# Index scores of a head pair in two groups of four, with a quarter tile of the projection between them

## The reference, cut to what matters

```
qi = rope_partial(split_heads(qi, N_IDX_HEADS), pos)
ki = rope_partial(ki[:, :, None], pos)[:, :, 0]
...
sc = jnp.einsum('thd,sd->ths', qi, ki) * IDX_DIM ** -0.5
score = jnp.einsum('ths,th->ts', jax.nn.relu(sc), w)
```

## Time and profile before

| what | us |
|---|---|
| median of three runs | 2710.42 |
| the three runs | 2716.11, 2710.42, 2710.17 |
| span of the profiled execution | 2720.3 |
| TensorE busy in it | 2572.7 |
| TensorE's mean granted clock | 0.975 |

### The profile page before, as it was taken

How to read it: one execution, slowest core, us unless ns; L and a number is a source line. 1 busy time by engine, 2 the same in 40 slices (tenths; PEclk the granted TensorE clock), 3 DMA queues, 4 the chain that set the end, 5 groups by cost and what they waited for, 6 DMA issues and landing times.

```text
span 2720.3 us, 52410 instructions
## 1 busy us (share of the span) xinstructions
PE 2572.7 (95%) x16711; PEld 2180.8 (80%) x16711; DVE 994.4 (37%) x1779; ACT 818.7 (30%) x1546; POOL 868.0 (32%) x651
## 2 busy tenths in 40 slices
PE   7999999999999999879999999999999999996997
PEld 2227879899999989779922388898999999896997
DVE  2241346776111234431103423487731122344113
ACT  0012334444333333322200133344433333333221
POOL 5012224334333333334300232343343333342341
PEclk8999999999999999989999999999999999998999
DMA  8983222223333323234478622232233333222443
GB/s 264 346 287 104 55 57 74 73 71 88 90 90 97 80 75 82 59 110 133 151 239 276 214 72 54 63 81 69 74 98 88 93 85 80 76 68 73 136 125 131
DMA packets 410102, 311.75 MB, mean 115 GB/s; under 512 B 21304, under 2 KB 347840, under 8 KB 408712
## 3 DMA queue, kind: packets, MB, share of 16 engines
q1 hardware_dynamic: 382296, 283.35, 35.8%
q10 hardware_dynamic: 27632, 26.21, 3.1%
HBM read 280.81 MB, written 30.92 MB: 115 GB/s over the span
## 4 chain that ended last, share of the span: by engine, by line
issue 56%; PE 20%; POOL 19%; POOLq 2%; DMA 1%; DVE 0%; SPq 0%; DVEq 0%; ACT 0%; ACTq 0%
POOL w_lo L458 18%; PE misc L513 6%; PE proj L572 4%; PE proj L566 4%; PE proj L568 4%; POOL act_lo L451 1%; POOLq L443 1%; POOLq L441 1%; POOLq L465 1%; POOLq L457 0%; PE misc L521 0%; DMA out_y_prompt<-work 0%; PE misc L489 0%; DVE work L1159 0%; DMA raw<-in_w_in 0%
## 5 line engine op out<-in xcount | busy, mean ns | idle before, releaser
L566 PE MATMUL proj<-act_hi,w_hi 128*128 128x288 f32 (+1 forms) x4672 | 1336.6, 301 | 29.2 <-DVE act_lo L1156 20.1
L568 PE MATMUL proj<-act_lo,w_hi 128*128 128x288 f32 (+1 forms) x4672 | 1312.1, 296 | 0.0
L458 POOL TENSOR_TENSOR w_lo<-raw,w_hi 128x512 fp32r<-128x512 f32 (+1 forms) x584 | 778.4, 1336 | 1432.6 <-ACT w_hi L866 1432.4
L572 PE MATMUL proj<-act_hi,w_lo 128*128 128x288 f32 (+1 forms) x4672 | 1004.1, 296 | 0.0
L566 PEld LDWEIGHTS proj<-act_hi,w_hi 128*128 128x128 f32 (+1 forms) x4672 | 883.1, 189 | 58.8 <-issue 48.0
L568 PEld LDWEIGHTS proj<-act_lo,w_hi 128*128 128x128 f32 (+1 forms) x4672 | 883.6, 189 | 3.4
L572 PEld LDWEIGHTS proj<-act_hi,w_lo 128*128 128x128 f32 (+1 forms) x4672 | 752.3, 188 | 0.0
L866 ACT ACTIVATE w_hi<-raw 128x512 fp32r<-128x512 f32 (+1 forms) x584 | 365.6, 629 | 1186.5 <-PE proj L572 1141.9
L513 PE MATMUL misc<-work,sc 128*2 128x512 f32 x768 | 344.8, 607 | 18.7 <-DMA work<-in_w_ada 11.5
L513 PEld LDWEIGHTS misc<-work,sc 128*2 128x2 f32 x768 | 64.2, 86 | 278.6 <-issue 278.3
L451 POOL TENSOR_TENSOR act_lo<-xy,act_hi 128x576 fp32r<-128x576 f32 x32 | 50.2, 1582 | 352.7 <-ACT act_hi L873 296.2
(11 more groups left out here) (169 smaller groups left out, 1695.0 us busy)
## 6 DMA issues: line engine op xcount, KB each, us to landing
raw<-in_w_in SPq DMA_DIRECT2D x448, 256.0 KB, 2.9
work<-in_w_ada SPq DMA_DIRECT2D x96, 1024.0 KB, 5.2
raw<-in_w_out SPq DMA_DIRECT2D x128, 256.0 KB, 2.8
x_keep<-xy ACTq DMA_DIRECT2D x32, 288.0 KB, 2.5
lb<-x_keep SPq DMA_DIRECT2D x24, 288.0 KB, 3.3
x_keep<-xy ACTq DMA_DIRECT2D x4, 1152.0 KB, 11.6
out_y_prompt<-work SPq DMA_DIRECT2D x4, 1024.0 KB, 3.9
qi_raw<-x_keep SPq DMA_DIRECT2D x8, 288.0 KB, 3.8
```

The lines of the kernel that those rows point to most:

```text
L458: pool.tensor_tensor(w_lo[:, c, :, 0:width], raw[:, c, :, 0:width], w_hi[:, c, :, 0:width].bitcast(F32), ALU.subtract)\
L566: pe.matmul(dst, w_hi[:, c, kk, 0:width], act_hi[:, k, cols], start=(k == 0), stop=False)
L568: pe.matmul(dst, w_hi[:, c, kk, 0:width], act_lo[:, k, cols], start=False, stop=False)
L572: m = pe.matmul(proj[b][0:width, half, 0:HALF], w_lo[:, c, kk, 0:width], act_hi[:, k, cols], start=False, stop=(k == KT - 1))
```

## The change

On TensorE alone, `scores` takes a half, products 0 to 3 or 4 to 7. In a query tile the swap product comes after the first quarter in place of the second. Then come two quarters, the first four products, the fourth quarter, and the last four products. In the first recurrent block the swap product stays after the second quarter, and the products are split in the same way around the fourth quarter. There are 8 pairs in each of 2 layers, so 16 places.

```diff
-                def scores(q, first=False):
+                def scores(q, half, first=False):
 
-                    hold(pe, roped, l * 17 + q + 2)
+                    if half == 0:
+                        hold(pe, roped, l * 17 + q + 2)
                     for e, (b, hh) in enumerate((b, hh) for b in (1, 2, 3, 4) for hh in range(2)):
+                        if e // 4 != half:
+                            continue
                         hold(pe, idx_read, l * 64 + (8 * q + e - 3 if not first or e > 3 else 0))
...
                 def query_tile(q, b, use, first=False):
 
-                    chunks(QI + q, b, use, (0, 1))
+                    chunks(QI + q, b, use, (0,))
                     swap(QI - 1 + q, 1 - b, swap_i[:, :], qi_raw, P)
-                    chunks(QI + q, b, use, (2, 3))
+                    chunks(QI + q, b, use, (1, 2))
                     if first:
                         hold(pe, ki_ready, l + 1)
                         hold(pe, t_read, l * T_EV + 2)
-                    scores(q - 1, first)
+                    scores(q - 1, 0, first)
+                    chunks(QI + q, b, use, (3,))
+                    scores(q - 1, 1, first)
...
                     if first:
                         swap(QI + 7, 0, swap_i[:, :], qi_raw, P)
-                    chunks(LRU + 2 * g, 1, g + 4, (2, 3))
+                    chunks(LRU + 2 * g, 1, g + 4, (2,))
                     if first:
-                        scores(7)
+                        scores(7, 0)
+                    chunks(LRU + 2 * g, 1, g + 4, (3,))
+                    if first:
+                        scores(7, 1)
                         hold(pe, idx_read, (l + 1) * 64)
                         t_event(2)
```

## The result

The changed kernel takes 2772.4 us (median of 4 runs, 2766.0 to 2775.2) against 2713.3 us. The ratio is 1.0208, with a 95% interval of 1.0188 to 1.0229. It is slower, as forecast. But the forecast was +39 us with a range up to 2765, and the time lies above that range. Run once more beside the kernel before, it gave 2770.3 against 2717.1 us, ratio 1.0199 (1.0183 to 1.0215), so +53 us. The spans of the profiled executions are 2770.2 and 2768.5 us after, 2720.3 and 2718.0 us before.

A forecast was written before the change was run, and what follows sets the result against it. TensorE's own stream was taken to bound the kernel. Four products 23.8, first tiles 4.5 and clock 11 summed to +39.3 us, giving 2750 us from the median 2710.4, range 2734 to 2765.

The forecast's parts named there:

- The bound: Whole kernel and index-query stages: TensorE's own stream sets the pace, busy 2572.7 of 2720.3 us.
- the tie of product 4 to the end of the fourth quarter: Query tile: product 4 still comes 2.64 us after the last matmul, through ScalarE's fourth upper, copy and first ReLU.
- the four products that lose their cover: Products 0 to 3, moved ahead of the fourth quarter, cost 1.49 us in each of 16 places, +23.8 us.
- The wait of the first tile: First query tile: earlier swap product waits 2.24 us for take_query(0), +4.5 us over two layers.
- The swap product: Steady query tiles: its earlier place costs 0 and gains nothing, since nothing waits for VectorE or the freed bank.
- The faster rival: First four ReLUs run during the fourth quarter, the 16.9 us of waits go away, 2700 us; chance 0.05.
- the clock's term: Gaps before product 4 and in first tiles: 10 clock falls out of 18 gaps at 1.1 us, +11 us.
- the discount from 1.56 to 1.1: A full low-clock stretch costs 1.56 us; taken as 1.1 for overlap with idle time and products 4 to 7.
- The rival with a fall at every gap: All 18 gaps bring the clock down at full price, 28 us, giving 2767 us; chance 0.12.
- the clock would have held: Rival, by the skill's rule: clock stays at 1.00 in the gaps, sum 28.3 us, 2739 us; chance 0.23.

The follow-up runs named there:

- e4_filled: Changed kernel with four matmuls on constant data filling the idle stretch in each of the 16 places; +27.6 us against before, ratio 1.0112.
- e7_first_filled: e1_swap_only with four matmuls on constant data in the wait before the first tile's swap product; +2.4 us against before, ratio 1.0011.
- e2_split_only: Changed kernel with the swap product back after the second quarter; +51.1 us against before, ratio 1.0204.
- e6_late_wait: e3_relus_ahead with swap product back after the second quarter, TensorE's wait for pair 7's ReLUs moved behind tile LRU+1; -19.7 us against before, ratio 0.9927.
- e3_relus_ahead: Changed kernel with ScalarE's first four ReLUs of a pair ahead of the fourth upper, last four behind the copy; -12.2 us against before, ratio 0.9956.
- e1_swap_only: Kernel before with the swap product after the first quarter, eight products together behind the fourth; +12.1 us against before, ratio 1.0047.
- e9_half_filled: e4_filled with two added matmuls in place of four in each place; +34.1 us against before, ratio 1.0135.
- after: The changed kernel, first measurement and profile; 2772.4 us against 2713.3, ratio 1.0208.
- after_again: The changed kernel once more, unaltered, for a second profile; +53.2 us against before, ratio 1.0199.
- before_again: The kernel before once more, unaltered, for a second profile; -1.3 us against before, ratio 0.9989.

## Why the prediction was right and wrong

**What held.** The bound, the tie of product 4 to the end of the fourth quarter (2.64 us before and after), and the four products that lose their cover. Their term was 23.8 us, and e4_filled and e7_first_filled give 2 x 11.88 = 23.8. The wait of the first tile was forecast as 2.24 us a layer and is 2.09 and 2.03. The swap product costs next to nothing else, 0.26 us in a layer. The prediction saw no gain in its earlier place either, but there is one once the products are split: e2_split_only and e6_late_wait show that the old place would have cost some 0.4 us a tile. The faster rival asked for ReLUs ahead of the fourth quarter's end. ScalarE's order excluded them in this change, and where that order was altered, in e3_relus_ahead, they brought the gain.

**What failed: the clock's term.** It was put at 10 falls by 1.1 us, 11 us in all. Measured, in each layer: 1.72 us behind the first tile (e1_swap_only against e7_first_filled), and behind the places the stage of the changed kernel, (166.10 + 172.23 + 170.23 + 169.28) / 4 = 169.46 us, less the 158.91 of e4_filled, so 10.55. Two layers by 12.27 make **24.5 us**. The sum is then 23.8 + 4.1 + 0.5 + 24.5 = 52.9 us, and the runs gave 59 and 53.

The count and the price were both too low. There are 13 gaps with a fall in one profile and 14 in the other, but some lasted two or three times as long, which makes 16 and 19 low stretches for the 10 assumed. One stretch costs about 1.5 us (1.47 behind the places, 1.72 in a first tile), and not 1.1. The step that failed is the discount from 1.56 to 1.1. It says that a low stretch overlaps "the idle time itself and products 4 to 7, which ScalarE paces". But hardly any of it lies in the idle time: in the two profiles of the changed kernel the low stretches begin between 0.4 us before product 4 and 1.4 us after it, for instance at 353.30 with product 4 at 353.43. And ScalarE's pace hides little: unpaced, products 4 to 7 take 1.81 us at the whole clock (e3_relus_ahead), paced 2.16, and at the low clock 3.68, twice the unpaced time. So the full price fell due, 3.61 - 2.09 = 1.52 us by the start of the next quarter.

The clock's term accounts for 13.5 of the 22 us that 2750 was short. With it the sum gives 2710.4 + 52.9 = 2763, which still lies inside the stated range. The other 9 us up to 2772.4 are 3 by which the kernel before came out higher in the comparison itself (2713.3) and 6 that the second comparison, at +53, does not show, and no run says where they lay. The rival with a fall at every gap had the better price, but its 2767 is under the measured time too. Its 18 low stretches are near the 16 and 19 of the traces, though these lie behind 13 and 14 gaps.

The Trainium skill, page "TensorE: Matmul & The Clock Gate", section "Why this matters for your kernels", advises against longer idle gaps than these, by which the clock would have held. The trace does not agree, and the measurement decides: idle stretches of 2.33 us between dense work brought the clock down in 11 and 12 of 16 places.

## What to carry to other kernels

Before moving work out of a wait, ask what ends the wait: if it is another engine's program order, the wait stays where it was and the moved work is simply added. Split both sides of a handshake or neither. And price a longer idle stretch of TensorE twice, once for itself and once for the clock behind it. Here the second was as dear as all the products moved, and matmuls that nobody needs, put in the gap, won back about half of the loss.

## What the runs showed of the hardware

- How the granted clock answers an idle stretch of TensorE that recurs between dense matmuls, in 16 places of a profile: 0.40 us brought no fall (e4_filled); 1.07 us none in the two profiles before, but for behind pair 7, where a second wait of 1.65 us follows and three of four were followed by a fall; 1.36 us one (e9_half_filled); 2.33 us 11 and 12, and 7 in e2_split_only. A single wait of 2.0 to 2.1 us in the first tile was followed by a fall in both layers each time (for instance in after, after_again and e1_swap_only), and one of 2.32 us in e3_relus_ahead in one layer of two.
- A low stretch that was filled with the products was in some places followed by a second one at 1.2 GHz, although TensorE was busy for 3.27 of the first 3.40 us (353.30 to 360.10 above). In others it was not: at 312.4 the same products ran just as long, 3.67 us, and the clock was whole again after 3.40.
- Where the products follow close behind the rotation that they wait for, the first four take 1.72 to 1.81 us for 1.35 (e2_split_only, e6_late_wait). I read it as TensorE's queue, which has five semaphore waits ahead of them and no lead left. No run took the waits apart, so this is argued and not shown.
- The same program differs by some 10 us between executions, and the granted clock goes with it: the 12 runs of before_again lie between 2707.6 us at a clock of 0.980 and 2721.2 us at 0.973. Spans of single profiles are a poor measure of changes under 0.5%.
